# One wide VectorE operation in place of two for the rest of each weight piece of the expert stages

## What is computed

```python
q = (xn @ w_pq).reshape(B, S, 8, 2, 128)
s1, s2 = q[..., 0, :] . sub_k1, q[..., 1, :] . sub_k2       # 128 keys each
...                                                        # top 16 of each, top 16 of the 256 sums, softmax: gates
eidx = e1 * 128 + e2                                       # 8 x 16 of 16384 experts for a token
act = gelu(einsum('tkd,td->tk', expert_u[eidx], xn))
h = h + einsum('tk,tkd->td', act * gates, expert_v[eidx])
```

## Time and profile before

| | |
|---|---|
| runs | 3005.99 us median of 3 (3005.98 to 3009.66) |
| profiled execution | 3007.15 us, span 3005.4 us |
| granted TensorE clock | 0.998 of full |
| TensorE matmul busy | 2962.8 us, 99% |
| TensorE weight load busy | 2678.9 us, 89% |
| VectorE busy | 2020.9 us, 67% |
| ScalarE busy | 1488.6 us, 50% |

### The profile page before, as it was taken

One profiled execution on the slowest core, in us unless ns is written; L12 is line 12 of the kernel. 1 busy time (PEld: TensorE's weight loads), 2 busy tenths in 40 slices (PEclk: granted clock), 3 DMA queues, 4 the chain that ended last, 5 costly groups with the idle time before them and its releaser, 6 DMA issues.

```text
span 3005.4 us, 42961 instructions
## 1 busy us (share of the span) xinstructions
PE 2962.8 (99%) x17085; PEld 2678.9 (89%) x17085; DVE 2020.9 (67%) x2869; ACT 1488.6 (50%) x2274; POOL 169.0 (6%) x312
## 2 busy tenths in 40 slices
PE   8999999999999999999999999999999999999999
PEld 7998778888888888978789999999999999999999
DVE  5656654444445445554557988888888888888876
ACT  4355544444444444454444466447745555555553
POOL 2000000000000002140000000000010000000000
PEclk9999999999999999999999999999999999999999
DMA  7554355556554554535667779778999899899764
GB/s 255 160 169 154 114 169 193 189 188 193 184 195 182 194 189 150 169 109 208 190 208 249 237 261 338 238 222 293 337 371 360 300 328 321 310 322 318 264 221 141
DMA packets 238382, 690.73 MB, mean 230 GB/s; under 512 B 14249, under 2 KB 95177, under 8 KB 203392
## 3 DMA queue, kind: packets, MB, share of 16 engines
q1 hardware_dynamic: 221024, 598.71, 59.2%
q0 software_dynamic: 12608, 71.73, 6.3%
q10 hardware_dynamic: 4576, 17.89, 1.6%
HBM read 652.61 MB, written 33.57 MB: 228 GB/s over the span
## 4 chain that ended last, share of the span: by engine, by line
PE 51%; DVE 0%; ACTq 0%; ACT 0%; issue 0%; DVEq 0%
PE banks L2156 16%; PE banks L2232 14%; PE banks L2157 8%; PE banks L2233 7%; PE banks L2203 2%; PE banks L2253 1%; PE banks L2255 1%; PE banks L2254 1%; PE banks L2175 0%; DVE peer_features L378 0%; DVE weights_lo L195 0%; PE banks L2192 0%; PE banks L2221 0%; ACTq L2310 0%; DVE residual L2585 0%; DVE peer_scratch L2584 0%
## 5 line engine op out<-in xcount | busy, mean ns | idle before, releaser
L195 DVE TENSOR_TENSOR weights_lo<-weights,weights_hi 128x1024 fp32r<-128x1024 f32 (+4 forms) x1080 | 1228.5, 1179 | 701.8 <-ACT weights_hi L188 700.0
L188 ACT ACTIVATE weights_hi<-weights 128x1024 fp32r<-128x1024 f32 (+4 forms) x1080 | 1046.4, 1017 | 1316.8 <-PE banks L419 640.8
L2156 PE MATMUL banks<-peer_features,weights_hi 128*128 128x448 f32 (+1 forms) x2304 | 738.9, 377 | 2.7 <-DVE weights_lo L195 2.7
L417 PE MATMUL banks<-weights_hi,features_hi 128*128 128x512 f32 (+3 forms) x1600 | 605.2, 378 | 12.5 <-DVE weights_lo L195 9.3
L2157 PE MATMUL banks<-peer_features,weights_lo 128*128 128x224 f32 (+1 forms) x2304 | 615.3, 267 | 0.0
L419 PE MATMUL banks<-weights_hi,features_lo 128*128 128x512 f32 (+3 forms) x1600 | 600.5, 375 | 0.0
L418 PE MATMUL banks<-weights_lo,features_hi 128*128 128x512 f32 (+3 forms) x1600 | 600.4, 375 | 0.0
L2232 PE MATMUL banks<-peer_features,weights_hi 128*128 128x448 f32 x1568 | 492.4, 374 | 0.0
L2156 PEld LDWEIGHTS banks<-peer_features,weights_hi 128*128 128x128 f32 x2304 | 432.0, 187 | 44.2 <-DVE weights_lo L195 3.2
L2157 PEld LDWEIGHTS banks<-peer_features,weights_lo 128*128 128x128 f32 x2304 | 438.6, 190 | 0.0
L2233 PE MATMUL banks<-peer_features,weights_lo 128*128 128x224 f32 x1568 | 414.3, 264 | 0.0
(11 more groups left out here) (406 smaller groups left out, 2757.7 us busy)
## 6 DMA issues: line engine op xcount, KB each, us to landing
weights<-in_expert_u SPq DMA_DIRECT2D x128, 1024.0 KB, 5.5
weights<-in_expert_v SPq DMA_DIRECT2D x128, 1024.0 KB, 7.2
weights<-in_w_ffn_gate SPq DMA_DIRECT2D x44, 1024.0 KB, 5.1
weights<-in_w_ffn_up SPq DMA_DIRECT2D x44, 1024.0 KB, 5.1
weights<-in_w_ffn_down SPq DMA_DIRECT2D x44, 1024.0 KB, 4.8
weights<-in_w_in SPq DMA_DIRECT2D x48, 900.0 KB, 4.7
weights<-in_w_out SPq DMA_DIRECT2D x32, 1024.0 KB, 5.1
weights<-in_w_in SPq DMA_DIRECT2D x24, 704.0 KB, 4.2
```

Of the source, the lines that this page charges most:

```text
L188: act.activation(hi[:, k, n], raw[:, k, n], ACT.Copy).then_inc(self.hi_ready, 1 + skip)
L195: last = dve.tensor_tensor(lo[:, k, n], raw[:, k, n], hi[:, k, n].bitcast(F32), ALU.subtract)
L417: pe.matmul(out, xh, wh, start=first, stop=False)
L2156: pe.matmul(self.bank(n % 3, 2 * (T - lo)), wh[:, k, :], F[:, k, :, lo:T], start=(k == 0), stop=False)
```

## The change

A new method of `Ring` makes the whole piece's `lo` in one operation of 2048 columns. It waits for both halves of `hi`. VectorE's loop over the expert stages calls it for all pieces from the third on, that is for 270 of 272. ScalarE still makes `hi` in two operations, and the counts of the semaphores are the same.

```diff
+    def split_lo_whole(self, dve, stream, i, j, half):
+
+        hi, lo, raw = self.piece(self.hi, half, stream), self.piece(self.lo, half, stream), self.raw(j, half, stream)
+        dve.wait_ge(self.hi_ready, i * 16 + (2 * (2 * (self.fills + j) + half) + 2))
+        dve.tensor_tensor(lo, raw, hi.bitcast(F32), ALU.subtract).then_inc(self.lo_ready, 1)
...
-                        ring.split_lo(dve, tiles, i, j, half)
+                        if s < 2:
+                            ring.split_lo(dve, tiles, i, j, half)
+                        else:
+                            ring.split_lo_whole(dve, tiles, i, j, half)
```

## The result

| | kernel before | changed kernel |
|---|---|---|
| median of 20 runs each, same chip, us | 3007.52 (3005.98 to 3011.25) | 3012.40 (3010.55 to 3014.31) |
| ratio of the times, 95% interval | 1 | 1.0015 (1.0008 to 1.0022) |
| span of the profiled execution, us | 3005.4 | 3008.9 |
| mean granted clock | 0.998 | 0.998 |
| VectorE busy, us | 2020.9 | 2002.0 |

The account below looks back on a forecast made before the run. TensorE was taken to bound the expert stages. Late pieces 2.00, spans' first pieces 0.75 and the change of stages 0.63 summed to 3.4 us, added to a median of 3005.99: 3009.4 us, range 3004.5 to 3015.

Parts of the forecast that it names:

- The bound: Expert stages: TensorE, busy without a gap, sets the time; its 2.7 us of waits for L195 lie at unchanged pieces.
- rival E: VectorE as the bound in places: 270 x 0.075 = 20 us less from fewer operations, 2986 us; chance 0.03.
- The wide operation: VectorE's 2048-column subtraction: 2.28 us long, 2.20 to 2.21 until the next, saving 0.075 us per piece.
- The ordinary piece: Pieces in the 5.01 us rhythm: no cost, but VectorE's slack before TensorE's load falls from 1.15 to 0.27 us.
- Rival B: Some 160 ordinary pieces wait if ready over 0.27 us later than forecast; 0.1 us excess costs 16, about 3026; chance 0.11.
- The late places: Five pieces where VectorE comes late behind L2532: 0.31, 0.24, 0.54, 0.52 and 0.39 us late, sum 2.00.
- The fifth: Late piece at 2369.15: 0.39 us late, or nothing if the scores' transfer lands at its old time.
- The change of stages: First piece of the value stage, last bank freed behind the next piece's L195: 0.63 us late, once.
- The spans' first pieces: 15 places where TensorE needs banks emptied by leave_sums behind L195: 0.05 us late each, 0.75 us in all.
- rival C: Weight refills come too late for ScalarE at a tenth of 256 expert pieces: 6 us more, 3015 us; chance 0.05.

Follow-up runs that it names:

- wait_alone: Changed kernel with the wait for both halves kept, but two operations of 1024 columns again: 3014.92 us against 3007.10 for the kernel before, ratio 1.0026.
- late_places_narrow: Changed kernel with the two-operation form given back at 25 pieces, at or ahead of late places: 3008.47 us against 3007.10 for the kernel before, ratio 1.0005.

## Why the prediction was right

**The bound.** Nothing was won on VectorE's 18.9 us: TensorE's waits of 2.7 us for L195 are still there, and rival E, faster by the count of operations, fell by 26 us. That is the grouping side of the Trainium skill's page Perfetto Trace Analysis, section Optimizing Scalar/DVE Operations: larger operations can help if the engine is saturated, and VectorE, 67% busy, wasn't. The other side of the same section, that breaking up instructions may then let work be completed sooner, holds here only together with the early wait: in two operations behind the late wait (wait_alone) the stages lost 6.18 us for 3.84, in two with the early wait at 25 pieces (late_places_narrow) 0.75. The page's some 60 ns per instruction stand beside 18.9 / 270 = 0.070 us measured here.

**The wide operation.** 2.28 forecast from L395, 2.292 measured (mean of 270), 2.20 until the next (2205.75 - 2203.54 = 2.21). The start came 0.03 us after ScalarE's pair.

**The ordinary piece.** Slack 0.27 forecast, 0.26 measured, and the two kernels with added delay put its edge where the subtraction of rows had it. Rival B did not come about in this kernel. Its mechanism and its point (more than 0.27 late) are those of the kernel with 0.4 us added, but its price was wrong: 160 x 0.1 should have been about half, since every second piece is let off.

**The late places.** Four of the five came within 0.05 us of the forecast (0.31, 0.24, 0.59, 0.51). Timeline at the first:

```profile
2207.19 2.02 DVE L2541 TENSOR_TENSOR normed<-normed,peer_rstd 128x1792 f32<-128x1792 f32 x1
2209.13 2.28 DVE L202 TENSOR_TENSOR weights_lo<-weights,weights_hi 128x2048 fp32r<-128x2048 f32 x1
...
2211.46 0.19 PEld L2162 LDWEIGHTS banks<-peer_features,weights_hi 128*128 128x128 f32 x1 [0.32 <-DVE weights_lo L202]
```

No bracket stands behind the two VectorE rows: it had no idle time and took over the lateness of the piece before. Where the forecast was 0.05 short, at piece 150, it is the way from end to load that was mis-sized:

```profile
2290.81 2.28 DVE L202 TENSOR_TENSOR weights_lo<-weights,weights_hi 128x2048 fp32r<-128x2048 f32 x1
...
2293.21 0.19 PEld L2238 LDWEIGHTS banks<-peer_features,weights_hi 128*128 128x128 f32 x1 [0.61 <-issue]
```

The end is at 2293.09 and the load 0.12 later, for 0.06 in the forecast (the bracket's "issue" means that the profile names no releaser). (Beside the second execution of before, which lost 0.28 here to a transfer, the change costs 0.3 at this place.) The fifth was the case that the prediction held open:

```profile
2369.18 2.02 DVE L2541 TENSOR_TENSOR normed<-normed,peer_rstd 128x1792 f32<-128x1792 f32 x1 [0.27 <-DMA normed<-expert_scores]
2371.91 2.29 DVE L202 TENSOR_TENSOR weights_lo<-weights,weights_hi 128x2048 fp32r<-128x2048 f32 x1 [0.71 <-ACT weights_hi L188]
...
2374.32 0.19 PEld L2238 LDWEIGHTS banks<-peer_features,weights_hi 128*128 128x128 f32 x1
```

The transfer did not move with VectorE, VectorE waited for ScalarE again behind it, and 0.06 was lost for 0.39. Sum of the five: 1.71 for 2.00.

**The change of stages.** 0.62 for 0.63. The load stood until L2443 behind the wide operation of piece 145 was done:

```profile
2264.23 2.29 DVE L202 TENSOR_TENSOR weights_lo<-weights,weights_hi 128x2048 fp32r<-128x2048 f32 x1 [0.98 <-ACT weights_hi L188]
2266.44 0.38 DVE L2443 TENSOR_TENSOR peer_scores<-banks,peer_rest 128x224 f32<-128x224 f32 x1
...
2266.88 0.19 PEld L2238 LDWEIGHTS banks<-applied_parts,weights_hi 128*128 128x128 f32 x1 [0.64 <-DVE peer_scores L2443]
```

**The spans' first pieces.** This is the term that was sized too small: 0.08 each on average and not 0.05, 1.20 us in all for 0.75.

```profile
2504.78 2.47 DVE L2471 TENSOR_TENSOR peer_scratch<-banks,peer_scratch 128x224 f32<-128x224 f32 x8
...
2504.97 0.19 PEld L2239 LDWEIGHTS banks<-peer_features,weights_lo 128*128 128x128 f32 x1
2505.27 0.19 PEld L2238 LDWEIGHTS banks<-peer_features,weights_hi 128*128 128x128 f32 x1
```

The first leave_sums ends at 2504.78 + 0.38 = 2505.16 and the load is at 2505.27, 0.11 later, where the forecast had taken 0.06 from L195. The loads are otherwise 0.21 apart at that point; here 0.30.

**What was missed.** Three more places, pieces 35, 106 and 216 (34, 105 and 215), lose 0.07 to 0.09 each, 0.24 in all. Together: 1.71 + 0.62 + 1.20 + 0.24 = 3.77, beside the shift of 3.84. **The sum of 3.4 was the right mechanism with one term too small (0.45), one too large (0.3) and 0.24 left out.** That the first two nearly cancel is luck. The median, 3.0 us above the forecast, stayed inside the range by its width: half of the 3.0 is the kernel before, whose three runs at the time of the forecast were low, and 1.0 is the part not located in the stages.

**The refills** (rival C). The densest stretch, line L148 from 2320 to 2400 us, after:

```profile
DMA to landing us min/median/max: 5.1/7.6/13.2
```

No slower than the earlier trace rows, and no L188 of the expert stages waits for a transfer. Rival C fell.

## What to carry to other kernels

An operation that saves an engine 0.07 us but may start only when its last input half is there costs the next engine what the start moved (0.95 us here), less the time saved (0.07) and whatever slack the hand-over had (1.15): look at slack, not at busy time, before merging across a producer's halves. It is then lost at the few places where the engine has no idle time to fall back on, and they can be found beforehand in the timeline, one by one: here 24 places among 272 pieces carried 3.77 of 3.84 us, and keeping two operations at 25 pieces took 3.1 of the 3.8 us away. And a hand-over left with 0.26 us of slack stands near an edge: 0.4 us more, which costs the old order 4.4 us, costs the new one 25.

## What the runs showed of the hardware

**One stream, two rhythms.** Pieces 6 to 15, the last ten of `w_pq`, with no wait of TensorE in them, take either 5.65 or 5.55 us each, and which one differs between executions of the same code: 5.65 in the first profile of before, 5.55 in its second. It can also change within one execution, at pieces 4 and 5, where TensorE has other work in between: from 5.65 to 5.55 in the second profile of before, the other way in that of the changed kernel. Stretches of TensorE (busy with its count of matmuls, clock, DMA share, GB/s), before and before once more:

```profile
1500.00:1550.00 50.00, 50.00 (x285) 1.00 0.67 215
```

```profile
1500.00:1550.00 50.00, 50.00 (x291) 1.00 0.69 212
```

The granted clock is 1.00 in both, the matmuls are the same, and the difference is spread over them in steps of at most 0.01 us. The changed kernel had each in one execution (290 and 285 matmuls in that stretch). From piece 6 on that is worth 10 x 0.10 = 1.0 us from run to run, a quarter of what was measured here. What sets it is open.

**A wait that is half repaid.** In the chain of ScalarE, VectorE and TensorE a wait of TensorE at one piece gives the next piece's VectorE that time, so a lateness common to all pieces costs only half of itself per piece (0.13 us short: 10.16 for two pieces, not 10.28). That holds where VectorE has idle time; at pieces 28 to 55, where it has hardly any, nearly every one lost 0.10.

**From VectorE's end to TensorE's load.** Where TensorE stood waiting, its load came 0.05 to 0.06 us after the end of VectorE's operation (2211.41 to 2211.46 at piece 134), and 0.12 after it in the spans where its program waits for two semaphores ahead of the piece (2293.09 to 2293.21 at piece 150).
